# A routing stage that ends with single-tile sets, issues the first record and gather, and splits the first expert's weights in a shared buffer

## The reference, cut to what matters

```python
x = layer_norm(DN_ALPHA * x + g1 * mix, ln1_g[l], ln1_b[l])   # mix = merged @ w_o
u2 = x * (1.0 + sc2) + sh2
aff = jax.nn.sigmoid((xf @ w_router).astype(jnp.float32))      # 16 experts in 4 groups
# sel = aff + b_router; best group by its two best experts; top 2 experts inside it
# gates = aff of the two, divided by their sum
# token copies sorted by expert, each expert's rows padded to blocks of 128 (MOE_BLOCK)
def expert_block(args):
    xb, e = args
    h = jax.nn.silu(xb @ w_gate[e]) * (xb @ w_up[e])
    return h @ w_down[e]
# results weighted by the gates and summed per token; final layer norm
```

## Time and profile before

| what | value |
|---|---|
| median of three runs | 2830.31 us |
| the profiled execution's own time | 2828.71 us |
| its span | 2827.1 us |
| granted TensorE clock, mean | 0.947 |
| TensorE, VectorE, ScalarE, POOL busy | 89%, 52%, 39%, 31% of the span |
| routing stage, first statistics to barrier | 1684 to 1959 us |
| expert stage | 1959 to 2765 us |

### The profile page before, as it was taken

How to read it: one execution, slowest core, us unless ns; L and a number is a source line. 1 busy time by engine, 2 the same in 40 slices (tenths; PEclk the granted TensorE clock), 3 DMA queues, 4 the chain that set the end, 5 groups by cost and what they waited for, 6 DMA issues and landing times. The chain is left out here.

```text
span 2827.1 us, 36325 instructions
## 1 busy us (share of the span) xinstructions
PE 2514.5 (89%) x12521; PEld 2096.9 (74%) x12522; DVE 1470.5 (52%) x1880; ACT 1115.0 (39%) x1814; POOL 862.7 (31%) x721
## 2 busy tenths in 40 slices
PE   5999799899999999999968969983998999999970
PEld 4788577788888888888857758773887888888760
DVE  6111165666565666565632356765446544526636
ACT  2111154554454545454520012112456545536633
POOL 2111044442222222222202225556222222323236
PEclk9999899999999999999989989995999999999985
DMA  7655687767666574747456546423467656636735
GB/s 262 244 183 186 177 270 228 226 213 222 199 200 195 198 224 158 212 146 209 141 192 223 167 157 225 149 97 120 132 186 231 208 147 174 209 87 202 258 74 238
DMA packets 254746, 534.87 MB, mean 189 GB/s; under 512 B 23412, under 2 KB 93160, under 8 KB 253992
## 3 DMA queue, kind: packets, MB, share of 16 engines
q1 hardware_dynamic: 232040, 468.39, 50.8%
q0 software_dynamic: 15248, 46.62, 7.7%
q10 hardware_dynamic: 7344, 18.35, 1.7%
HBM read 380.26 MB, written 153.02 MB: 189 GB/s over the span
## 5 line engine op out<-in xcount | busy, mean ns | idle before, releaser
L92 PE MATMUL mx_acc<-u_u,mx_w_hi 128*128 128x512 f32 x1792 | 570.9, 400 | 3.3 <-DMA mx_w_lo<-halves 3.3
L659 POOL TENSOR_TENSOR mx_wt<-mx_wt,mx_rest 128x127 f32<-128x127 f32 (+15 forms) x128 | 271.4, 2120 | 701.2 <-DVE mx_rest L864 701.2
L92 PEld LDWEIGHTS mx_acc<-u_u,mx_w_hi 128*128 128x128 f32 x1792 | 325.9, 190 | 67.9 <-DMA mx_w_lo<-halves 4.1
L872 DVE TENSOR_TENSOR mx_wt_lo<-mx_p_t,mx_wt_hi 128x512 fp32r<-128x512 f32 (+2 forms) x320 | 192.3, 605 | 332.3 <-ACT mx_wt_hi L825 330.4
L92 PE MATMUL mx_acc<-u_u,mx_w_lo 128*128 128x512 f32 x896 | 352.9, 394 | 0.0
L825 ACT ACTIVATE mx_wt_hi<-mx_p_t 128x512 fp32r<-128x512 f32 (+2 forms) x320 | 170.9, 534 | 400.2 <-PE mx_p_t L713 354.7
L864 DVE TENSOR_TENSOR_SCAN mx_rest<-mx_rest,mx_zero 128x128 f32<-128x128 f32 (+15 forms) x128 | 319.2, 2493 | 14.6 <-ACT mx_wt L807 14.6
L92 PE MATMUL moe_p_gu<-moe_gu_hi,moe_x_hi 128*128 128x512 f32 x656 | 263.5, 402 | 15.1 <-DVE moe_gu_lo L1840 13.0
L92 PE MATMUL moe_p_gu<-moe_gu_hi,moe_x_lo 128*128 128x512 f32 x656 | 259.0, 395 | 0.0
L92 PE MATMUL moe_p_gu<-moe_gu_lo,moe_x_hi 128*128 128x512 f32 x656 | 258.8, 395 | 0.0
L713 PE MATMUL mx_p_t<-keep_ident,mx_wt 128*128 128x128 f32 x1088 | 175.6, 277 | 37.7 <-POOL mx_wt L659 29.0
(11 more groups left out here) (242 smaller groups left out, 5248.4 us busy)
## 6 DMA issues: line engine op xcount, KB each, us to landing
mx_w_hi<-halves SPq DMA_DIRECT2D x84, 512.0 KB, 4.0
mx_w_lo<-halves SPq DMA_DIRECT2D x84, 512.0 KB, 5.4
keep_stay<-in_w_gate SPq DMA_DIRECT2D x64, 512.0 KB, 5.7
keep_stay<-in_w_up SPq DMA_DIRECT2D x64, 512.0 KB, 6.5
keep_stay<-in_w_down SPq DMA_DIRECT2D x32, 1024.0 KB, 6.4
u_saved<-u_u SPq DMA_DIRECT2D x4, 4096.0 KB, 19.2
mx_w_mod<-in_w_ada SPq DMA_DIRECT2D x64, 256.0 KB, 5.4
gate_t<-mx_g_out SPq DMA_DIRECT2D x64, 256.0 KB, 5.1
```

What stands on the lines that cost most here:

```text
L92: mm = pe.matmul(out, a, b, start=first and n == 0, stop=last and n == len(pairs) - 1, skip_group_check=True)
L659: pool.tensor_tensor(wt[:, t % 2, 0:w - 1], wt[:, t % 2, 0:w - 1], rest[:, t % 2, 1:w], ALU.mult).then_inc(m["weights_done"], 1)
L872: dve.tensor_tensor(wt_lo[:, first:first + k - j], p_t[:, n % TR, 0:(k - j) * P].rearrange("p (j t) -> p j t", t=P), f32(wt_hi[:, first:fi ...
```

## The change

What it does:

- The last two tiles are sets of their own. Set 3 (tiles 12, 13) is chosen in step 14, set 4 (tile 14) in step 15, set 5 (tile 15) in step 16. `put` has its own table `PLACE_AT`. The affinities of tile 14 are taken by ScalarE in step 15 behind the normalisation.
- `rank` runs after k = 3 instead of after `logits` at k = 5; the sum of rows uses another PSUM column range and waits for the last affinities only.
- Scatters have tables: tiles 0 to 3 one a step (8 to 11), tiles 4, 5 in step 12, tiles 6, 7 in step 13, tiles 8, 9 behind the products for `x1t` of step 14, tiles 10, 11 before those of step 15, tiles 12 to 15 behind them.
- POOL, at the end of the routing block, loads the start row of block 0, waits for all scatters, issues the record load and, when the rows of u2 are stored and the record is in, the gather of block 0. The expert block no longer does.
- `w_hi`, `w_lo` of the routing stage and `gu_hi`, `gu_lo` of the experts are one pair of buffers (`wide`), and y of the routing stage is `x_raw` of the experts. ScalarE makes the eight high chunks of expert 0 at the end of the routing block, VectorE the first four low chunks behind `block_row`; the other four follow in the expert block, two before `low_x(0)` and two behind it.
- TensorE turns block 0 first and transposes the zeros after it. SP waits for the first gather before it loads expert 1.

```diff
-    SETS = ((0, 4), (4, 8), (8, 12), (12, 14), (14, 16))
+    SETS = ((0, 4), (4, 8), (8, 12), (12, 14), (14, 15), (15, 16))
-    CHOOSE_AT = {5: 0, 9: 1, 13: 2, 16: 3, 17: 4}
-    RANK_AT = {7: 0, 11: 1, 15: 2, 17: 3, 18: 4}
+    CHOOSE_AT = {5: 0, 9: 1, 13: 2, 14: 3, 15: 4, 16: 5}
+    RANK_AT = {7: 0, 11: 1, 15: 2, 16: 3, 17: 4, 18: 5}
+    PLACE_AT = {7: 0, 11: 1, 14: 2, 15: 3, 16: 4, 17: 5}
+    SCATTER_AT = {8: (0,), 9: (1,), 10: (2,), 11: (3,), 12: (4, 5), 13: (6, 7), 15: (10, 11)}
+    SCATTER_LATE = {14: (8, 9), 15: (12, 13, 14, 15)}
...
-        w_hi, w_lo = s.sb("w_hi", [P, KD, D], F32R), s.sb("w_lo", [P, KD, D], F32R)
+        w_hi, w_lo = wide
+        gu_raw, record = expert_raw(stay)[0].rearrange("p k g f -> p k (g f)"), first["record"]
...
-        y, x1t = s.sb("y", [P, D]), s.sb("x1t", [P, 2, D])
+        y, x1t = first["x_raw"], s.sb("x1t", [P, 2, D])
...
+                        if k == 3 and t in RANK_AT:
+                            rank(RANK_AT[t])
                         if k == 5:
                             logits(t - 2)
-                        if k == 5 and t in RANK_AT:
-                            rank(RANK_AT[t])
...
-            pe.wait_ge(m["rank_used"], len(SETS))
-            pe.matmul(p_r[:, 1, 0:E], ones[:], seen[:, NT], start=True, stop=True).then_inc(m["ranked"], 1)
+            pe.wait_ge(m["aff_done"], len(SETS))
+            pe.matmul(p_r[:, 0, 0:E], ones[:], seen[:, NT], start=True, stop=True).then_inc(m["ranked"], 1)
...
+                if t == NT - 1:
+                    affinities(NT - 2)
...
+            act.wait_ge(m["mix_done"], NT)
+            for k in range(KD):
+                if k % PIECE == 0:
+                    act.wait_ge(ahead["piece"][k // PIECE], 32)
+                act.activation(w_hi[:, k], gu_raw[:, k], ACT.Copy).then_inc(m["gu_hi_done"], 1)
...
-                scatter_at(t)
...
+                for late in SCATTER_AT.get(t, ()):
+                    scatter(late)
+                pool.wait_ge(m["u2_half"], t + 1)
+                pool.tensor_tensor(x1t[:, t % 2], x1t[:, t % 2], ln_g[:], ALU.mult).then_inc(m["x1_step"], 1)
+                pool.wait_ge(m["x1_step"], t + 1)
+                pool.tensor_tensor(x1t[:, t % 2], x1t[:, t % 2], ln_b[:], ALU.add).then_inc(m["x1_done"], 1)
+                for late in SCATTER_LATE.get(t, ()):
+                    scatter(late)
+            pool.wait_ge(m["row_set"], 1)
+            start = pool.value_load(block_row[0:1, 0:1], min_val=0, max_val=E * CAP)
+            pool.wait_ge(m["record_set"], 1)
             pool.wait_ge(m["scattered"], 32 * NT)
+            pool.dma_start(record[:, 4], records[bass.ds(start, P), :]).then_inc(ahead["record_in"], 16)
+            for i in range(UR):
+                pool.wait_ge(u2_stored[i], 16 * len(range(i, NT, UR)))
+            pool.wait_ge(m["normed"], NT)
+            pool.wait_ge(ahead["record_in"], 16)
+            pool.indirect_dma_start(out=first["x_raw"][:], out_offset=None, in_=u2_rows,
+                                    in_offset=bass.IndirectOffsetOnAxis(ap=record[:, 4, 0:1], axis=0)
+                                    ).then_inc(ahead["x_in"], 16)
...
-                if t in RANK_AT:
-                    put(RANK_AT[t])
+                if t in PLACE_AT:
+                    put(PLACE_AT[t])
...
+            for k in range(LO_AHEAD):
+                dve.wait_ge(m["gu_hi_done"], k + 1)
+                dve.tensor_tensor(w_lo[:, k], gu_raw[:, k], f32(w_hi[:, k]), ALU.subtract).then_inc(m["gu_lo_done"], 1)
...
+            sp.wait_ge(m["x_in"], 16)
             with sp.Fori(1, E) as e:
...
-            pool.memset(record[:], 0).then_inc(m["record_set"], 1)
             pool.memset(h[:], 0.0).then_inc(m["zeros_set"], 1)
-            pool.wait_ge(m["record_set"], 1)
-            load_record(0)
-            gather_x(0)
...
+            turn_x(0)
             pe.wait_ge(m["zeros_set"], 1)
...
-            turn_x(0)
             with pe.Fori(0, E) as e:
...
-            split_gu(0, None)
             high_x(0)
...
-            split_gu(0, None)
+            split_gu(0, 0, range(LO_AHEAD, LO_AHEAD + 2))
             low_x(0)
+            split_gu(0, 0, range(LO_AHEAD + 2, KD))
```

More of the change, by code:

```diff
@@ L1404, in scatter @@
                                             ).then_inc(m["scattered"], 16)
[L1406 to L1416, removed]
[L1417 to L1421 removed]
+            pool.memset(record[:], 0).then_inc(m["record_set"], 1)
+            for t in range(NT):
+                past(pool, m["normed"], t)
+                pool.wait_ge(m["var_done"], t + 1)
+                pool.tensor_scalar(var[:], mv[:, 1:2], EPS, None, ALU.add).then_inc(m["var_step"], 1)
+                pool.wait_ge(m["var_step"], 2 * t + 1)
+                pool.tensor_tensor(rstd[:], var[:], minus_half[:], ALU.pow).then_inc(m["var_step"], 1)
+                pool.wait_ge(m["var_step"], 2 * t + 2)
+                pool.tensor_scalar(offset[:], mv[:, 0:1], rstd[:], -1.0, ALU.mult, ALU.mult
+                                   ).then_inc(m["rstd_done"], 1)
                 if t == 0:
@@ L1608, in experts @@
         gu_raw, dn_raw = expert_raw(stay)
-        gu_hi, gu_lo = s.sb("gu_hi", [P, KD, 2, FF], F32R), s.sb("gu_lo", [P, KD, 2, FF], F32R)
+        gu_hi, gu_lo = (w[:].rearrange("p k (g f) -> p k g f", g=2) for w in wide)
         dn_hi, dn_lo = s.sb("dn_hi", [P, KF, D], F32R), s.sb("dn_lo", [P, KF, D], F32R)
-        x_raw = s.sb("x_raw", [P, D])
+        x_raw, record = first["x_raw"], first["record"]
         x_hi, x_lo = s.sb("x_hi", [P, KD, P], F32R), s.sb("x_lo", [P, KD, P], F32R)
@@ L1783, in split_gu @@
                         act.wait_ge(piece_in[c // PIECE], 32 * e + 32)
[L1784 to L1785 removed]
+                    act.wait_ge(m["gu_used"], done * KD + (c + 1))
                     act.activation(hi, raw, ACT.Copy).then_inc(m["gu_hi_done"], 1)
@@ L1832, in _, with split_gu @@
             dve.sem_inc(m["y_free"], 3)
+            dve.sem_inc(m["gu_lo_done"], LO_AHEAD)
             dve.sem_inc(m["dn_lo_done"], KF)
-            def split_gu(e, done):
-                for c in range(KD):
+            def split_gu(e, done, chunks=range(KD)):
+                for c in chunks:
                     raw, hi, lo = chunk(c)
@@ L2015, in hybrid_layer @@
         }
-        ahead = {"w_o": [s.sem(f"w_o{k}") for k in range(KD)], "piece": [s.sem(f"piece{i}") for i in range(PIECES)]}
+        ahead = {"w_o": [s.sem(f"w_o{k}") for k in range(KD)], "piece": [s.sem(f"piece{i}") for i in range(PIECES)],
+                 "record_in": s.sem("record_in"), "x_in": s.sem("x_in")}
         with ExitStack() as uctx:
@@ L2026, in hybrid_layer @@
         branch_outputs(nc, used, keep, stay, ahead, conv_t, o_t, gate_t, w_a, w_b, w_o, m_t)
-        mix_norm_route(nc, used, keep, stay, ahead, w_gate, w_up, w_down, m_t, x, mod_rows, ln1_g, ln1_b, w_router, b_router,
+        wide = tuple(s.sb(n, [P, KD, D], F32R) for n in ("wide_hi", "wide_lo"))
+        first = {"record": s.sb("record", [P, 5, 2], U32), "x_raw": s.sb("x_raw", [P, D])}
+        mix_norm_route(nc, used, keep, stay, ahead, wide, first, w_gate, w_up, w_down, m_t, x, mod_rows, ln1_g, ln1_b, w_router, b_router,
                        acc, u2_rows, records)
```

35 lines of the change are left out of this document (13 added, 22 removed).

## The result

The kernel after took 2836.97 us (median of 15 runs, 2831.53 to 2840.67), the kernel before 2829.4 us beside it (15 runs). The ratio is 1.0027, 95% interval 1.002 to 1.0034: slower by 7.6 us, where 6.6 us less were forecast. The profiled execution of after took 2839.4 us with a span (first to last instruction) of 2837.8 us, 10.7 us more than the span of before.

What follows compares the result with a forecast made beforehand. TensorE, busy throughout the expert loop, was taken as the bound, so an earlier first expert product ends the kernel as much earlier: 9.7 - 2.1 - 1.0 = 6.6 us off, 2823.7 us for the median, range 2818.5 to 2828.5.

Steps and rivals of the forecast that it cites:

- Value nothing either way: Expert 0's weight splits, moved from under the gather to under the scatters' landing, were to gain or lose nothing.
- the slower one (the late second gather): Rival: second record and gather queue behind the weight loads, landing at 1989; 12.7 us lost, 2833.3 us; chance 0.08.
- Ranks: Routing steps 7, 11 and 15: rank moved ahead of TensorE's stall; steps 7 and 11 together 0.7 us earlier, step 15's lost.
- Sets and the port: Routing stage's end: single-tile sets, slowed by POOL's products holding VectorE's port, give block_row at 1952.9, 2.6 us later.
- the forecast's 4.7: Inside tile 14's set, POOL's multiplication and addition for tile 15 were to block VectorE twice, 4.7 us in all.
- Record, gather, first product: Hand-over to the experts: record at 1955.5, gather 1958.4, x 1963.3, first product 1968.5, which is 9.7 us gained.
- The drain: the rival: Rival at the routing block's end: POOL's drain waits for the gather, everything behind it 3.3 us later, 2827.0 us; chance 0.15.
- nothing more: Taken for POOL's drain at the routing block's end: no longer than 2.93 us with a gather in flight.
- a drain beyond 3 us: Sign that the prediction is wrong: POOL's drain lasting beyond 3 us.
- The second gather: Expert stage's second gather: issued at 1977.5, landed 1982.4, now late for TensorE; 2.1 us lost and 1.0 of clock.
- a first-block wait above 4 us: Sign that the prediction is wrong: a wait above 4 us in the first expert block.

Runs made afterwards that it cites:

- b1_gap_64: The kernel before with an unused 64-byte buffer behind the low halves of the weights in the routing and expert stages: 2840.74 us, ratio 1.0042.
- a3_record_ahead: The kernel after with the `record` buffer allocated ahead of all the others: 2826.87 us, ratio 0.9994 to the kernel before.
- b2_all_shifted_64: The kernel before with a 64-byte gap ahead of all buffers of these stages, so operand distances stay: 2828.84 us, ratio 1.0005.
- a4_clear_late: a3_record_ahead with POOL's clears of dn_hi and dn_lo moved behind the issue of the second gather: 2820.44 us, ratio 0.9968 to the kernel before.
- a5_weights_after_second: a4_clear_late with SP starting expert 1's weight loads after the second gather instead of the first: 2820.13 us, ratio 0.9973 to the kernel before.
- a6_gather_late: a3_record_ahead with the first record load and gather back in the expert block, behind the barrier: 2831.12 us, ratio 1.0009 to the kernel before.
- the three kernels with a gap: The kernel before with an unused buffer: b1_gap_64, b2_all_shifted_64, and one with 128 bytes where b1_gap_64 has 64 (2839.92 us, ratio 1.0038).
- a4_again: The unchanged kernel of a4_clear_late run once more, beside a5_weights_after_second on the same chip: 2820.58 us, ratio 0.9975 to the kernel before.

## Why the prediction was wrong

**The failed step: the one that isn't in the sum.** The prediction costed the shared weight buffers by what their splits do ("Value nothing either way") and gave the new allocation no term at all; with "a first expert product that starts n us earlier ends the kernel n us earlier, unless a new wait appears in the loop" it took the products' pace in the loop as given. It wasn't: 64 bytes between the wide buffers and the rest slow each gate and up product by 0.0066 us, without a wait. From x(2) to x(41) that is 10.6 us, shown by b1_gap_64 and undone by a3_record_ahead (some 10.4 us each, with the clock near x(11) taken out). No rival had it; the slower one (the late second gather) got the sign right with another cause. The Trainium skill (SBUF — State Buffer, "Who interferes with whom") says that TensorE waits on no other engine, and its table gives TensorE two read ports, one for the moving operand and one for weight loads, independent of each other. By that the term would be nothing. The runs say otherwise, and they decide: 0.2333 us a product against 0.2267, by the distance between the two operands alone.

**Ranks: not shown.** 0.7 us were forecast. Between the transposes of tile 5 and of tile 13 a3_record_ahead gains 0.5 us, and b2_all_shifted_64, which has the old ranks, 0.6.

**Sets and the port: the mechanism right, the exact sum luck.** Two additions of a few elements inside tile 14's set met POOL's products. Timeline of VectorE in the kernel after:

```profile
1935.48 2.63 DVE L1532 TENSOR_TENSOR mix_g_key<-mix_g_score,mix_top 128x4 f32<-128x4 f32 x1
...
1938.34 0.16 DVE L1534 TENSOR_REDUCE mix_top<-mix_g_key 128x1 f32<-128x4 f32 x1
1938.53 2.01 DVE L1535 TENSOR_TENSOR mix_g_off<-mix_g_key,mix_top 128x4 f32<-128x4 f32 x1
...
1955.46 0.20 DVE L1620 CAST keep_block_row<-mix_p_t 1x54 int32<-1x54 f32 x1 [0.46 <-PE mix_p_t L1317]
```

2.63 and 2.01 us for 4 elements a partition, 4.3 us more than the same two take in tile 15's set (0.16 each): the forecast's 4.7. The reduction, with one input, passes in 0.16 beside the second product. One input alone is no safeguard: a cast of 8 elements took 1.68 us at 1915.37 beside POOL's product for tile 14 (1913.64 to 1917.03). block_row was forecast for 1952.9 and came at 1955.46; less the 2.56 us that this execution was late at tile 13, 1952.9. That is luck in part: on the same footing the last norm started 0.9 us later than forecast (1923.1 for 1922.2), and shorter sets and a shorter tail made it up.

**Record, gather, first product: right within 1 us, with two misses that cancel.** Less the same 2.56: record 1954.8 (forecast 1955.5), gather 1957.6 (1958.4), turn of x 1964.0 (1963.3), first product 1968.9 (1968.5). The gather landed 4.35 us after its issue, half a microsecond under the 4.85 taken, which brings x forward; the drain, below, puts it back. The fit of the Trainium skill (DMA: Bandwidth & Descriptors, "Anatomy of one DMA") gave an estimate of 3.2 us for these 512 KB, and the trace does not agree.

**The drain: the rival was true.** The prediction took "nothing more" and named a drain beyond 3 us as a sign of being wrong. The drain of 6.14 us ended 1.57 us after the gather had landed (1964.50), and TensorE's turn of x waited for the barrier (PEq), not for x. That cost 2.0 us at x(0), from the landing to the turn at 1966.52; with the gather issued 0.8 us earlier and landing 0.5 us quicker than forecast, 0.7 of it shows. It also held back POOL's clears and with them the second record, by 1.1 us against the forecast (barrier at 1963.7 for 1962.6).

**The second gather: the mechanism right, the size not.** Forecast: issue 1977.5, landing 1982.4, 2.1 us lost and 1.0 of clock. Measured, less the offset: issue 1979.5, landing some 1984. The record took the slow 5.8 us that the first had taken under load, and not the middle between the ends. From the first product to x(2) before needed 30.73 us (1978.22 to 2008.95), after 37.10 (1971.49 to 2008.59): 6.4 lost, some 0.6 of it pace, so 5.8 where 3.1 stood in the sum. TensorE's two waits are 4.4 us of it (the prediction had 2.1, and named a first-block wait above 4 us as a sign of being wrong). The clock is some 1.4: 0.50 over 4 us and 0.66 over the next 4 is 3.4 us of full-speed work not done, but before lost 2.0 in its own slow stretch, the 4 us from the first product on at half clock. The prediction had 1.0 for it and saved 0.5. The loss between x(0) and x(2) is 6.1 us in a3_record_ahead, 5.2 and 4.0 in the two runs of a4_clear_late's kernel, and nothing in a5_weights_after_second.

**The sum, corrected,** for the profiled execution: +2.6 from ahead of the hand-over, -10.2 up to x(0), +7.3 up to x(2) and +10.6 in the loop make +10.3, the ledger's value at x(41). Without the distance, a3_record_ahead, the forecast of 6.6 us would still have been 4 to 5 us too good, and the second gather is where they went.

## What to carry to other kernels

An allocation is part of a change. When a new buffer is put between others, compare the spacing of the same products in both traces before anything else; if it differs at the same clock and with no wait, restore the distance between streamed and stationary operand (here by allocating the small buffer ahead of the large ones). When a critical transfer is brought forward, look at the next one of its kind: it keeps its cover only if what stands before it on its engine, here a drain and 7 us of clears, comes forward too, and if it doesn't fall among large loads that used to be over by then. Bringing the clears out of its way alone left a wait of 2.1 to 2.8 us; moving the loads behind it as well left none. And POOL's drain at the block's end lasted until 1.57 us past the landing of the gather it had in flight, so work that must start early does not belong behind such an end.

## What the runs showed of the hardware that was not expected

- The pace of fp32r products of 512 columns depends on the distance in bytes within the partition between the buffers of the moving and the stationary operand. At the distances of before and of a3_record_ahead, all multiples of 4096 bytes: 17.72 or 17.73 us a block. 64 bytes more: 18.00. 128 bytes more: 17.94. A common shift of all buffers by 64 bytes changes nothing. That 4096 is the step that counts is not shown: no distance between 128 bytes and 4096 was tried, and a smaller step would fit as well. The distance between dn_hi and h_hi was a multiple of 4096 before, after and in b1_gap_64, and their products kept 0.227 us. Why the distance matters no run shows.
- POOL's drain at this block's end is 2.93 us when its software DMAs have landed (before, a6_gather_late and the three kernels with a gap) and 6.00 to 6.21 us with a gather in flight (the seven other traces), and in each of those seven it ends 1.57 us after the gather has landed.
- Beside weight loads a record load of 1 KB was issued 5.7 to 6.9 us ahead of its gather, without them 2.8 to 3.4. The first two gathers of 512 KB landed in 4.2 to 4.7 us with few or no loads beside them, and with loads beside them in 7.5 to 8.8 (the first of before and of the kernels with a gap, the second of a4_clear_late and a4_again).
